# A chunked recurrent scan on one Trainium2 core: 64x64 quarters of the matmul array in place of zero-padded 128x128 operands, and a chunk's inversion issued independently of the state

## What is computed

```python
def _wkv7_scan(s0, r, w, k, v, a, b):
    def step(s, inp):
        r_t, w_t, k_t, v_t, a_t, b_t = inp
        sa = jnp.einsum('bhij,bhj->bhi', s, a_t)
        s = (s * w_t[:, :, None, :] + sa[..., None] * b_t[:, :, None, :]
             + v_t[..., None] * k_t[:, :, None, :])
        return s, jnp.einsum('bhij,bhj->bhi', s, r_t)
```

## Time and profile before

| | |
|---|---|
| median of 3 runs | 2359.48 us (2359.03 to 2367.6) |
| the profiled execution's own time | 2365.84 us |
| its span in the profile | 2363.9 us |
| mean granted TensorE clock | 0.938 of full speed |
| the scan, from its first transpose to `pc` | 302.4 to 832.0 us, 529.6 us |

### The profile page before, as it was taken

The page is one execution under the profiler, slowest core; times in us unless marked ns, Lnnn a source line. Parts: engine busy times, 40 slices in busy tenths (PEclk is TensorE's granted clock), DMA queues, the critical chain, the costliest instruction groups (busy, mean ns, idle before and its releaser), DMA issues.

```text
span 2363.9 us, 33008 instructions
## 1 busy us (share of the span) xinstructions
PE 2109.4 (89%) x12995; PEld 1847.7 (78%) x12995; DVE 1330.1 (56%) x2206; ACT 563.5 (24%) x903; POOL 515.6 (22%) x496
## 2 busy tenths in 40 slices
PE   5999999999997699799899998799769797999985
PEld 3777689999996356589899898577447697998985
DVE  5237355656656842278358274589960785383563
ACT  2213232322222020233122121311021332122222
POOL 0000000000000000124444443079200244344440
PEclk8999899999999877999899999899879899999998
DMA  4022000000000030212322221221021122222221
GB/s 130 27 63 72 19 10 1 10 1 10 1 10 1 0 87 27 59 37 71 89 72 79 82 69 48 75 64 34 0 64 45 45 71 83 79 75 85 72 63 47
DMA packets 228490, 116.90 MB, mean 49 GB/s; under 512 B 26065, under 2 KB 226217, under 8 KB 228233
## 3 DMA queue, kind: packets, MB, share of 16 engines
q1 hardware_dynamic: 228377, 115.31, 17.2%
HBM read 109.33 MB, written 6.67 MB: 49 GB/s over the span
## 4 chain that ended last, share of the span: by engine, by line
PE 61%; DVE 22%; issue 12%; ACT 3%; DVEq 1%; DMA 1%; POOL 0%; ACTq 0%; SPq 0%; POOLq 0%
PE ps L462 25%; PE ps L717 20%; PE ps L543 15%; DVE arena L1606 6%; DVE arena L1523 2%; DVE arena L1519 1%; DVE arena L1528 1%; DVE arena L1502 1%; DVE arena L1356 1%; ACT hidsplit L1074 1%; DVE tmp L1410 1%; DVE tmp L1166 1%; DVE arena L1503 1%; DVE tmp L1427 1%; DVE arena L1522 1%
## 5 line engine op out<-in xcount | busy, mean ns | idle before, releaser
L1644 POOL TENSOR_TENSOR wsplit<-arena,wsplit 128x1024 fp32r<-128x1024 f32 x136 | 325.1, 2391 | 1403.5 <-ACT wsplit L1044 1403.5
L717 PE MATMUL ps<-hsplit,wsplit 128*128 128x288 f32 x4224 | 579.2, 299 | 20.5 <-POOL wsplit L1644 18.8
L717 PEld LDWEIGHTS ps<-hsplit,wsplit 128*128 128x128 f32 x4224 | 572.0, 191 | 26.3 <-POOL wsplit L1644 21.2
L462 PE MATMUL ps<-arena 128*128 128x288 f32 (+4 forms) x2048 | 523.8, 420 | 18.3 <-ACT arena L1131 6.5
L462 PEld LDWEIGHTS ps<-arena 128*128 128x128 f32 (+4 forms) x2048 | 396.0, 194 | 145.0 <-issue 25.9
L543 PE MATMUL ps<-arena 128*128 128x128 f32 (+2 forms) x2992 | 392.2, 285 | 48.4 <-DVE arena L1356 14.5
L543 PEld LDWEIGHTS ps<-arena 128*128 128x128 f32 x2992 | 359.9, 194 | 77.3 <-DVE arena L1356 19.3
L717 PE MATMUL ps<-hidsplit,wsplit 128*128 128x288 f32 x2112 | 297.6, 305 | 48.5 <-DVE hidsplit L1532 48.5
L717 PEld LDWEIGHTS ps<-hidsplit,wsplit 128*128 128x128 f32 x2112 | 295.6, 197 | 49.9 <-DVE hidsplit L1532 49.9
L1044 ACT ACTIVATE wsplit<-arena 128x1024 fp32r<-128x1024 f32 x136 | 138.9, 1051 | 224.8 <-PE ps L717 214.0
L1606 DVE SCALAR_TENSOR_TENSOR arena<-arena,par 128x512 f32<-128x512 f32 x322 | 174.7, 622 | 0.1
(11 more groups left out here) (191 smaller groups left out, 1847.4 us busy)
## 6 DMA issues: line engine op xcount, KB each, us to landing
arena<-ffn_w_in SPq DMA_DIRECT2D x88, 512.0 KB, 3.9
arena<-ffn_w_out SPq DMA_DIRECT2D x32, 512.0 KB, 4.1
arena<-conv_w_in SPq DMA_DIRECT2D x16, 512.0 KB, 4.0
arena<-ffn_w_out SPq DMA_DIRECT2D x16, 384.0 KB, 3.3
arena<-rwkv_wk SPq DMA_DIRECT2D x8, 512.0 KB, 5.7
arena<-rwkv_wr SPq DMA_DIRECT2D x8, 512.0 KB, 4.0
arena<-rwkv_wv SPq DMA_DIRECT2D x8, 512.0 KB, 4.1
arena<-rwkv_wo SPq DMA_DIRECT2D x8, 512.0 KB, 5.0
```

What stands on the lines that cost most here:

```text
L462: ins = pe.matmul(ps[0:m, o:o + HALF], lhs, rhs[:, HALF * z:HALF * z + HALF], start=st, stop=sp)
L717: ins = pe.matmul(ps[:, s + 512 * z:s + 512 * z + HALF], lhs(u, i), rhs[:, v, i, HALF * z:HALF * z + HALF], start=i == 0 and n == 0, stop= ...
L1644: p.tensor_tensor(wsplit[:, at % 4, 1], ring[:, at % 2], wsplit[:, at % 4, 0].bitcast(F32), ALU.subtract)\
```

## The change

**Quarters.** `both` (L557 of the changed kernel) replaces `mm`: for each pair it issues two matmuls, one on partitions 0 to 63 and one on 64 to 127, each with 64 rows, 64 columns of weights and 64 streamed columns, with results on the same half of PSUM's partitions. There are no zero blocks left: every operand is dense, 64 columns per pair in place of 128, and each eviction of four pairs is 128x256 in place of 128x512. The copies of `blocks` and the zeroing are gone; PE reads `ag`, `kb`, `kkb`, `rb`, `vb` directly, and transposes by multiplying with an identity (`front2`, `front4`).

**Order.** `front1` to `front4` are the factors and the token forms of a chunk. `TT`, the masked factors (`MB`, `MK`), the token forms (`BK`) and `VT` have two buffers each, so that `front1`, `front2` and `levels` of chunk c need nothing of the state. The residual, deltas and outputs of chunk c-1 are issued among the fronts of chunk c, before its levels. Each step has its own pair of semaphores.

**Samples.** The products with the sample states are per sequence: 128 matmuls with 64x64 weights and 16 streamed columns, which give each row its own state alone, so that mask and sum on DVE go. The state update stays 512 columns wide (L740), in halves; POOL makes one of its masked operands and does the final multiplication by the decay. The transposes of the sample states at the start stand between the chunks (`turn_states`, L673); those of the final states (`st`) stand behind `pc`. `Sd` lies in `ring`, so the loads of `wo` wait until `st` is done; `p_wkv` is stored in 4 pieces.

```diff
-            eng.wait_ge(sm["snat_ready"], 1)
+            for g in range(2):
+                eng.wait_ge(W[g]["su_done"], 4)
...
+            eng.wait_ge(sm["tile_full"], TB["st"] + 1 + KT)
             for j in range(RING):
                 wtile(WB["wo"] + j, a["rwkv_wo"][0], j)
...
+            def both(g, b, o, i, terms, w=64):
+                at = 2048 * g + 512 * b + o + w * i
+                for n, (lhs, rhs) in enumerate(terms):
+                    for e in (0, 64):
+                        ins = pe.matmul(ps[e:e + 64, at:at + w], lhs[e:e + 64], rhs[e:e + 64], start=n == 0, stop=n == len(terms) - 1)
+                return ins
...
+            def front1(g, c):
+                for i, k in enumerate(pairs(g)):
+                    both(g, 0, 0, i, [(ag[:, k, toks(c)], kkb[:, k, toks(c)])])
+                    ins = both(g, 0, 256, i, [(ag[:, k, toks(c)], rb[:, k, toks(c)])])
+                ins.then_inc(W[g]["f1_done"], 1)
...
+            def front2(g, c):
+                if c:
+                    pe.wait_ge(W[g]["tt_ready"], 6 * c)
+                for i, k in enumerate(pairs(g)):
+                    both(g, 1, 0, i, [(kkb[:, k, toks(c)], ag[:, k, toks(c)])])
+                    ins = both(g, 1, 256, i, [(vb[:, k, toks(c)], eye)])
+                ins.then_inc(W[g]["f2_done"], 1)
...
+            def level_y(g, c, n):
+                pe.wait_ge(W[g]["tt_ready"], 6 * c + n)
+                if n == 1:
+                    pe.wait_ge(W[g]["mn_ready"], c + 1)
+                for i, k in enumerate(pairs(g)):
+                    ins = both(g, 0, 0, i, [(Mn[:, k, :], TT[c % 2][:, k, :])])
...
+            def level_t(g, c, n, last):
+                pe.wait_ge(W[g]["yv_ready"], 5 * c + n)
+                pe.wait_ge(W[g]["ti_ready"], 5 * c + n)
+                if n == 1:
+                    pe.wait_ge(W[g]["vt_ready"], c + 1)
+                for i, k in enumerate(pairs(g)):
+                    ins = both(g, 1, 0, i, [(TI[:, k, :], Y[:, k, :])])
+                    if not last:
+                        ins = both(g, 1, 256, i, [(Y[:, k, :], TI[:, k, :])])
+                ins.then_inc(W[g]["t_done"], 1)
...
+            def levels(c):
+                top = len(LEVELS) if c < NCH else DLEV
+                for n in range(1, top):
+                    for g in range(2):
+                        level_y(g, c, n)
+                    if c == NCH:
+                        for g in range(2):
+                            (front3 if n == 1 else front4)(g, c)
+                    elif n < 5:
+                        (front3 if n < 3 else front4)((n - 1) % 2, c)
+                    for g in range(2):
+                        level_t(g, c, n, n == top - 1)
...
+            def deltas(g, c, adds):
+                pe.wait_ge(W[g]["rm_ready"], c + 1)
+                pe.wait_ge(W[g]["tt_ready"], 6 * c + adds)
+                for i, k in enumerate(pairs(g)):
+                    ins = both(g, 2, 256, i, [(TT[c % 2][:, k, :], Rm[:, k, :])])
+                ins.then_inc(W[g]["sa_done"], 1)
+            def residual(g, c):
+                pe.wait_ge(W[g]["mk_ready"], c + 1)
+                if c:
+                    pe.wait_ge(W[g]["s_ready"], c)
+                for i, k in enumerate(pairs(g)):
+                    terms = [(kkb[:, k, toks(c)], S[:, k, :])] if c else []
+                    ins = both(g, 2, 0, i, terms + [(MK[c % 2][:, 0, k, :], VT[c % 2][:, k, :])])
+                ins.then_inc(W[g]["r_done"], 1)
...
+            def outputs(g, c):
...
+                pe.wait_ge(W[g]["sav_ready"], c + 1)
+                pe.wait_ge(W[g]["bk_ready"], c + 1)
...
+                p = c % 2
+                for i, k in enumerate(pairs(g)):
+                    both(g, 2, 0, i, [(BK[p][:, 0, k, :], SA[:, k, :]), (BK[p][:, 1, k, :], VT[p][:, k, :])])
+                    terms = [(SA[:, k, :], MB[p][:, k, :]), (VT[p][:, k, :], MK[p][:, 1, k, :])]
+                    if c:
+                        terms.append((S[:, k, :], rb[:, k, toks(c)]))
+                    ins = both(g, 3, 256, i, terms)
+                ins.then_inc(W[g]["sy_done"], 1)
...
+            for c in range(NCH + 1):
                 if c:
-                    pe.wait_ge(y_read[g], c)
+                    residual(0, c - 1)
+                    residual(1, c - 1)
+                front1(0, c)
+                front2(0, c)
+                if c:
+                    deltas(0, c - 1, len(LEVELS))
+                    deltas(1, c - 1, len(LEVELS))
+                front1(1, c)
+                front2(1, c)
+                if c:
+                    outputs(0, c - 1)
+                    outputs(1, c - 1)
+                levels(c)
+                if c >= 2 and c % 2 == 0:
+                    turn_states(c // 2 - 1)
...
+                        at = 2048 * g + P * i + 16 * b
+                        for e in (0, 64):
+                            ins = pe.matmul(ps[e:e + 64, at:at + 16], Sd[e:e + 64, k, 64 * b:64 * b + 64], ARd[e:e + 64, k, 16 * b:16 * b + 16],
+                                            start=i == 0 and b == 0, stop=False, skip_group_check=True)
...
+                    ins = both(g, 2, 0, i, [(WA[:, k, :], eye), (MK[0][:, 0, k, :], VT[0][:, k, :])])
...
+                    o = ps[:, 2048 * g + P * i:2048 * g + P * i + P].rearrange("p (b x t) -> p b x t", x=2, t=DS)[:, :, 1, :]
+                    for lhs, rhs in ((VT[0][:, k, :], MK[0][:, 1, k, :]), (SA[:, k, :], MB[0][:, k, :])):
+                        for e in (0, 64):
+                            ins = pe.matmul(o[e:e + 64], lhs[e:e + 64], rhs[e:e + 64].rearrange("p (b t) -> p b t", t=DS),
+                                            start=False, stop=False, skip_group_check=True)
+                ins.then_inc(W[g]["sy_done"], 1)
...
+                    pe.wait_ge(W[g]["bk_ready"], c + 1)
+                    pe.wait_ge(W[g]["sam_ready"], i + 1)
+                    pe.wait_ge(W[g]["vm_ready"], i + 1)
+                    if i >= 2:
+                        pe.wait_ge(W[g]["sd_added"], i - 1)
+                    at = 2048 * g + 512 + 1024 * (i % 2)
+                    for n, (lhs, rhs) in enumerate(((BK[0][:, 0, k, :], SAm[:, 2 * g + i % 2, :]), (BK[0][:, 1, k, :], Vm[:, k, :]))):
+                        for e in (0, 64):
+                            ins = pe.matmul(ps[e:e + 64, at:at + 512], lhs[e:e + 64], rhs[e:e + 64], start=n == 0, stop=n == 1)
+                    ins.then_inc(W[g]["su_done"], 1)
...
                 product(TB["pc"] + kt, [(con[:, C_CEN:C_CEN + P], yg[:, kt, :], [])])
+            transposes(TB["st"], [S[:, 2 * k:2 * k + 2, :].rearrange("p k n -> p (k n)") for k in range(4)])
+            for k in range(KT):
+                pe.wait_ge(W[k // 4]["sd_final"], k % 4 + 1)
+                transposes(TB["st"] + 1 + k, [Sd[:, k, P * q:P * q + P] for q in range(DB // 2)])
...
-            def blocks(dst, src, k, tok):
-                for e in (0, 64):
-                    ins = f(dst[e:e + 64, k, e:e + 64], src[e:e + 64, k, tok], ACT.Copy)
-                return ins
...
+            def natural(g, c):
+                act.wait_ge(W[g]["f2_done"], c + 1)
+                f(Mn[:, four(g), :], quant(g, 1, 0), ACT.Copy).then_inc(W[g]["mn_ready"], 1)
+                f(VT[c % 2][:, four(g), :], quant(g, 1, 256), ACT.Copy).then_inc(W[g]["vt_ready"], 1)
...
+            def start_tt(g, c):
+                k, p = four(g), c % 2
+                dve.wait_ge(W[g]["f1_done"], c + 1)
+                seq(v.tensor_tensor(TT[p][:, k, :], quant(g, 0, 0), mask4(C_LVL), ALU.mult))
+                seq(v.tensor_tensor(MB[p][:, k, :], quant(g, 0, 256), mask4(C_MASK if c < NCH else C_MASKD), ALU.mult))
+                after()
+                v.tensor_tensor(TT[p][:, k, :], TT[p][:, k, :], mask4(C_IS), ALU.add).then_inc(W[g]["tt_ready"], 1)
...
+            def level_y(g, c, n):
+                dve.wait_ge(W[g]["y_done"], 5 * c + n)
+                v.tensor_tensor(Y[:, four(g), :], quant(g, 0, 0), mask4(C_LVL + 64 * n), ALU.mult).then_inc(W[g]["yv_ready"], 1)
+            def level_t(g, c, n, last):
+                k, p = four(g), c % 2
+                dve.wait_ge(W[g]["t_done"], 5 * c + n)
+                dve.wait_ge(W[g]["tt_ready"], 6 * c + n)
+                v.tensor_tensor(TT[p][:, k, :], TT[p][:, k, :], quant(g, 1, 0), ALU.add).then_inc(W[g]["tt_ready"], 1)
+                if not last:
+                    dve.wait_ge(W[g]["ti_ready"], 5 * c + n)
+                    v.tensor_tensor(TI[:, k, :], TI[:, k, :], quant(g, 1, 256), ALU.add).then_inc(W[g]["ti_ready"], 1)
...
+            def new_state(g, c):
...
+                dve.wait_ge(W[g]["sy_done"], c + 1)
+                decay = pend[:, k, c:c + 1].to_broadcast([P, 4, 64])
+                if c:
+                    dve.wait_ge(W[g]["s_ready"], c)
+                    seq(v.tensor_tensor(S[:, k, :], S[:, k, :], quant(g, 2, 0), ALU.add))
+                    after()
```

(46 more changed lines are left out.)

543 lines of the change are left out of this document (178 added, 365 removed).

## The result

The changed kernel takes 2129.9 us (median of 4 runs, 2127.91 to 2131.83), against 2360.24 us before (median of 4). The ratio worked out from all these runs is 0.9017, with a 95% interval of 0.8997 to 0.9037 (the medians alone give 0.9024): 230 us less. The profiled execution's own time is 2129.0 us, its span 2127.2 us.

What follows compares the result with a forecast made beforehand. It took the prompt's scan to be bound by PE's number of passes times their spacing. Its terms, 253.4 + 14.0 + 28 - 1.4 + 7.5 = 301.5 us for 529.6, gave a forecast of 2131 us, range 2105 to 2395.

Steps and rivals of the forecast that it cites:

- The spacing of the passes (30 ns), the deciding term: Scan and samples on PE: 8448 64-column passes start 30 ns apart if two quarters run side by side, 253.4 us.
- in turn: Rival for the quarter passes: the two quarters alternate, spacing 58.5 to 62 ns; 2381 us at 60 ns; chance 0.22.
- stops of 14 + 1.5 + 2.5: PE stalls in the prompt's scan: 14 us in seven chunks (2.0 each), 1.5 in the first, 2.5 in the ninth.
- transposes of 4.3 us: Between the chunks: 32 transposes of the sample states on PE, 4.3 us, counted among the stalls.
- The samples' products: Samples' stage: 416 small passes at 30 ns, plus 5.5 us stalls for the chain of products, residual, deltas and masks.
- the update: Samples' state update: 64 passes of 512 columns, in halves side by side, 14.0 us (28.0 if in turn).
- The start: Start of the scan: PE idles 2.3 us while ACT makes the last copies; 1.4 us taken off.
- the stretch behind `pc`: After the samples: `pc` first, then nine tiles of 4 transposes with ACT copies; adds 7.5 us.
- the likeliest case: Whole kernel with quarters side by side: 2131 us, its own range 2105 to 2185; chance 0.50.
- partial overlap: Rival: streams side by side but loads partly one after another, spacing 34 to 55 ns; 2244 us at 44; chance 0.13.
- The clock rival: Rival: granted clock falls to half, side-by-side passes double; 2381 us, or 2256 if for half the stretch; chance 0.15.
- its cover: Fronts issued while deltas and outputs wait for state copies; without them PE stops 1.4 us a chunk, 11 in all.

Runs made afterwards that it cites:

- the first two experiments: Changed kernel with each step's matmuls reordered, one half's all before the other's: 2259.66 us; changed kernel with eight groups of 128 extra passes ahead of the first chunk: 2174.18 us.
- the sixth experiment: Changed kernel with the final states' transposes moved behind both head sums and the head sum `pb` put first behind `pc`: 2125.93 us, ratio 0.8998.
- the second experiment: Changed kernel with eight groups of 128 extra passes (different quarters, full weights, last 16 streamed columns) ahead of the first chunk; one run, 2174.18 us, time not compared.

## Why the prediction was right

**The spacing of the passes (30 ns), the deciding term.** It measured 29.2 ns, and the first two experiments show the cause as the prediction put it: a quarter needs 58 to 59 ns for a pass, the bound worked out for taking turns, and two quarters share that time. It had only half of the chances because no row of before showed two quarters at work. The reason given (no common rows, columns or PSUM partitions) was more than it needs: sharing rows, or columns, costs nothing at this size either. The Trainium skill, "TensorEngine Tiling (Array Packing)", Key Properties, says that tiles load and multiply in parallel: 29 ns in place of 59 agrees. The bank rule of Gotcha 1 (PSUM Pressure) on that page of the Trainium skill, by which the prediction would have had the quarters in turn (the first of its rivals, which it calls the second there), does not reach this layout: in one bank on different partitions and in two banks, 126 passes took the same 3.84 us. The bound of some 62 ns per MATMUL that "TensorE: Matmul & The Clock Gate" of the Trainium skill gives for hardware decode off (section "Wait — 56ns, not 53.3ns?") is not in force here: a matmul of the program, two passes, starts every 58 ns, and every 30 with four quarters in turn.

**The sum, term by term.** Up to the samples: 8032 passes at 30 and stops of 14 + 1.5 + 2.5 and transposes of 4.3 us were to be 263.3; measured 256.3, of which the passes take 234.5, the transposes 4.1, and 17.7 are left for the stops, where 18.0 stood. Within that, a steady chunk lost about 1.9 us (two chunks from 421.92 to 482.81 in the chain, 30.4 each, less 960 x 29.2 ns and 0.5 for the transposes), as foretold, and the ninth more than its 2.5: POOL's contention alone, which the prediction took for hidden, was worth 1.8 there. The samples' products were to take 12.5 + 5.5 = 18.0 and took 18.6, the update 14.0 and took 15.0. The start saved 1.6 (1.4 foretold), the stretch behind `pc` cost 5.2 (7.5 foretold).

That the forecast of 2131 came within 1 us of the median is partly luck. In the two profiles, from the idle start to the gate products, 236 us were saved (555.4 to 319.4) where the sum had 228, mostly because a pass took 29.2 and not 30 ns. The medians fell by 230 all the same: the profiled execution of before was 5.6 us above its median, that of the changed kernel 0.9 below. Where the other 6 us went in the other executions no trace shows; the stages behind the gate products alone differ by 8.6 us between executions (the sixth experiment). The range of the likeliest case was also worked out loosely: its own figures give 2110 and 2182, not 2105 and 2185.

**The rivals.** In turn and partial overlap are excluded by the 29.2 ns. The clock rival came true in one small place: the granted clock was 1.00 through all chunks but 0.63 in the 18.6 us of the samples' products. It fell early in the 256 small passes:

```profile
554.10:555.90 1.80, 1.80 (x63) 1.80 (x64) 0.00 (x0) 0.00 (x0) 0.00 (x0) 1.00 0.04 9
556.00:566.30 10.30, 10.30 (x200) 10.30 (x198) 0.00 (x0) 0.38 (x1) 0.00 (x0) 0.50 0.01 2
```

The first 63 of them came 29 ns apart, the other 193 (555.9 to 566.1) 53 ns, and the 64 behind them 54 ns. At 29 ns these would have been 4.6 and 1.6 us shorter, about 6 us in all. So the term came out right by luck: 5.5 us had been set aside for waits, and almost all of it went to the clock. The prediction's ground for this rival, that rows in use stand beside the fall, does not hold. The 58.1 us window of the earlier trace rows had passes of 128 rows among those of 16 and 32:

```profile
L462 PE MATMUL ps<-hg,arena 128*128 128x288 f32 x24 | 13.7, 727 | 0.0
```

And here passes of 64 rows stood beside either level.

**The new order** was worth 14 us of 230; the prediction gave its cover 11 us by itself, near enough.

## What to carry to other kernels

Where products are 64 on a side, a zero-padded 128x128 pass does two blocks in 115 to 117 ns, and two quarter passes do them in 58; issue the quarters next to each other in the queue and they run at once, be they diagonal, in the same rows or in the same columns. Order matters at the grain of single matmuls: the same work in blocks of 8 to 40 per quarter lost 130 of the 230 us. And a link of another engine in the chain of waits is not idle time of the bound engine: before paying for its removal, count that engine's instructions between the same points of two rounds and compare with their steady spacing.

## What the hardware showed that I had not expected

Four quarters in turn ran at 15 ns a pass for 121 passes, then PE stopped for 0.79 us; whether 15 ns can be sustained was not tried. Two quarters with common rows or common columns run as freely as two on the diagonal.

The granted clock fell during passes of 64 rows and 16 streamed columns, in the samples' stage and in the second experiment, where all seven groups before had had 1.00. Windows of that kernel: the full-size passes, the first and the last of the 16-column ones, the changed kernel's first fronts behind them, and what follows:

```profile
324.10:338.50 14.40, 14.40 (x129) 14.33 (x129) 0.00 (x0) 0.00 (x0) 0.00 (x0) 1.00 0.01 2
338.60:341.20 2.60, 2.60 (x92) 2.60 (x94) 0.00 (x0) 0.00 (x0) 0.00 (x0) 1.00 0.00 0
341.50:343.00 1.50, 1.50 (x34) 1.50 (x33) 0.00 (x0) 0.00 (x0) 0.00 (x0) 0.50 0.04 11
343.10:348.20 5.10, 5.10 (x102) 5.10 (x102) 2.03 (x5) 0.66 (x2) 0.00 (x0) 0.51 0.00 0
348.30:352.00 3.70, 3.59 (x123) 3.48 (x121) 3.19 (x8) 0.66 (x2) 0.00 (x0) 1.00 0.02 4
```

PE was busy without a gap through the 16-column passes, so it was not idleness. The clock fell to its lower level of 1.2 GHz in the last third of them and stayed there under the 64-column passes behind, which started four in 0.213 us (53 ns each), and it is back at 1.00 in the last row.

DVE instructions with both operands in SBUF took up to three times as long while POOL ran (1.26 us for 0.42); those that read PSUM did not (0.41 us).
